# Retention's output blocks: group norm and gate product split over VectorE, ScalarE and GpSimd

## The reference, cut to what matters

```python
def head_groupnorm(y):
    mu = jnp.mean(y, axis=-1, keepdims=True)
    var = jnp.mean(jnp.square(y - mu), axis=-1, keepdims=True)
    return (y - mu) * lax.rsqrt(var + EPS)
...
    y, r_new = retention(q, k, vr, r0, chunk)
    y = head_groupnorm(y).reshape(B, T, R_V_WIDTH).astype(h.dtype)
    b = jax.nn.silu(gr) * y
```

## Time and profile before

| | |
|---|---|
| median of 3 runs | 1591.9 us (1589.27 to 1594.05) |
| the profiled execution's own time | 1587.36 us |
| its span | 1585.8 us |
| TensorE busy | 1550.2 us, 98% |
| VectorE busy | 882.9 us, 56% |
| ScalarE busy | 270.4 us, 17% |
| GpSimd busy | 62.9 us, 4% |
| output blocks, layer 0 | 357.4 to 414.6 us |
| output blocks, layer 1 | 1133.9 to 1191.1 us |

### The profile page before, as it was taken

The page is one execution under the profiler, slowest core; times in us unless marked ns, Lnnn a source line. Parts: engine busy times, 40 slices in busy tenths (PEclk is TensorE's granted clock), DMA queues, the critical chain, the costliest instruction groups (busy, mean ns, idle before and its releaser), DMA issues.

```text
span 1585.8 us, 24952 instructions
## 1 busy us (share of the span) xinstructions
PE 1550.2 (98%) x10010; PEld 1067.3 (67%) x10010; DVE 882.9 (56%) x1832; ACT 270.4 (17%) x556; POOL 62.9 (4%) x107
## 2 busy tenths in 40 slices
PE   6999999999999989999999999999999999999997
PEld 3999887775797544444449999886649965444443
DVE  2776864665752634344458768556485535434436
ACT  3110000112200421111131100011121033111111
POOL 0000000001001100000000000000010011000000
PEclk9999999999999999999999999999999999999999
DMA  9834665688843899999984437537886457999993
GB/s 396 334 111 160 261 271 226 268 342 329 334 160 113 317 366 422 420 421 421 422 352 153 161 142 286 193 127 307 335 342 249 160 224 275 416 419 421 422 420 138
DMA packets 49811, 461.43 MB, mean 291 GB/s; under 512 B 5968, under 2 KB 6224, under 8 KB 10144
## 3 DMA queue, kind: packets, MB, share of 16 engines
q1 hardware_dynamic: 44656, 414.38, 65.9%
q10 hardware_dynamic: 3456, 37.75, 5.7%
q0 software_dynamic: 1584, 7.69, 1.2%
HBM read 415.88 MB, written 43.91 MB: 290 GB/s over the span
## 4 chain that ended last, share of the span: by engine, by line
PE 86%; issue 8%; DMA 2%; DVE 1%; ACT 1%; POOL 1%; SPq 0%; POOLq 0%; DVEq 0%; ACTq 0%
PE ps L810 86%; DMA ring<-stream 1%; DMA ovd<-sorted_rows 1%; DMA sorted_rows<-work,packed_rows 1%; ACT work L1292 0%; POOL kzm L751 0%; POOL rstd L719 0%; POOL sorted_rows L771 0%; DVE rope L1611 0%; DVE hT L2187 0%; POOLq L718 0%; SPq L685 0%; DVEq L1555 0%; ACT hT L1292 0%; ACT modp L1292 0%
## 5 line engine op out<-in xcount | busy, mean ns | idle before, releaser
L810 PE MATMUL ps<-work,ring 128*128 128x144 f32 (+1 forms) x2624 | 358.2, 298 | 0.0
L810 PEld LDWEIGHTS ps<-work,ring 128*128 128x128 f32 x2624 | 341.0, 190 | 13.6 <-DVE ring L1653 0.2
L810 PE MATMUL ps<-ring,work 128*64 128x512 f32 x1472 | 323.9, 595 | 1.4 <-ACT work L1292 1.4
L810 PEld LDWEIGHTS ps<-ring,work 128*64 128x64 f32 x1472 | 106.6, 137 | 202.5 <-issue 202.4
L1292 ACT ACTIVATE work<-ps 128x256 f32<-128x256 f32 (+5 forms) x228 | 97.2, 433 | 720.9 <-PE ps L810 679.9
L810 PE MATMUL ps<-ring,hT 128*32 128x128 f32 (+2 forms) x1776 | 169.9, 312 | 3.0 <-ACT hT L1292 3.0
L810 PE MATMUL ps<-hT,ring 128*128 128x144 f32 (+1 forms) x1024 | 165.6, 317 | 0.0
L810 PEld LDWEIGHTS ps<-hT,ring 128*128 128x128 f32 x1024 | 145.8, 190 | 16.6 <-issue 3.6
L810 PE MATMUL ps<-work 128*128 128x288 f32 (+3 forms) x608 | 152.1, 393 | 3.4 <-DVE hT L2161 2.6
L810 PEld LDWEIGHTS ps<-ring,hT 128*32 128x32 f32 (+1 forms) x1776 | 126.1, 132 | 39.4 <-issue 26.5
L810 PEld LDWEIGHTS ps<-work 128*128 128x128 f32 (+1 forms) x608 | 100.6, 185 | 54.0 <-issue 26.9
(11 more groups left out here) (224 smaller groups left out, 1129.6 us busy)
## 6 DMA issues: line engine op xcount, KB each, us to landing
ring<-stream SPq DMA_DIRECT2D x194, 1024.0 KB, 10.4
ring<-stream SPq DMA_DIRECT2D x95, 2048.0 KB, 8.7
state_sample_out<-ring ACTq DMA_DIRECT2D x16, 2048.0 KB, 7.4
state_out<-prm ACTq DMA_DIRECT2D x8, 512.0 KB
work<-sorted_rows SPq DMA_DIRECT2D x6, 512.0 KB, 6.5
prm<-params SPq DMA_DIRECT2D x1, 2608.5 KB, 27.5
prm<-params POOLq DMA_DIRECT2D x1, 2608.5 KB, 16.7
cst<-consts SPq DMA_DIRECT2D x1, 1651.0 KB, 20.8
```

The source lines that it names most:

```text
L810: return nc.tensor.matmul(out, lhsT, rhs, start=start, stop=stop, **k)
```

## The change

VectorE keeps the statistics of all nine blocks and no longer multiplies out of PSUM. GpSimd's `inverse_root` also computes `centre` = -mean * rstd, with one more instruction ahead and one more, behind a second drain, at its end. ScalarE computes y * rstd + centre out of PSUM into `normal` (the buffer `modp`, two halves in turn) in `normalise`, and this is now what frees the block's bank. GpSimd multiplies the gate by that in `gate_rows` for n = 3 to 9; VectorE does it for the last two (n = 10 and 11), behind ysum's statistics. `inverse_root(n)` waits until block n-2 was normalised. `normalise(n)` waits until block n-2's gate product is done and, for n = 11, also block 10's.

```diff
--- before.py
+++ after.py
@@ -351,6 +351,7 @@
 VARS = 3 + 2 * HEADS + 1
 LN_DONE = 3
 B_DONE = 2 * HEADS + 1
+BY_VECTOR = LN_DONE + 2 * HEADS - 1
 NORMS = 2 * DEPTH
 SAMPLES = slice(SEQ, TOK)
 TTILES = ((0, P), (1, P), (2, NS))
@@ -383,6 +384,7 @@
         stats = sb("stats", [P, 2, 6])
         moments = sb("moments", [P, 4, 2])
         rstd = sb("rstd", [P, 2])
+        centre = sb("centre", [P, 2])
         kz = sb("kz", [P, 2, DK])
         scT = sb("scT", [P, 3, P])
         kzs = sb("kzs", [P, DK])
@@ -445,6 +447,16 @@
         sums_u = sums_of(work[:, QK_AT + 12 * RIDE:QK_AT + 12 * RIDE + KT * TOK], KT // 2, RIDE)
         sums_b = sums_of(work[:, SG_AT:SG_AT + 2 * KT * TOK], KT, RIDE)
         rope_flat = rope.rearrange("p a t -> p (a t)")
+        normal = modp
+
+        def normed_of(l, n):
+
+            head, c = (n - LN_DONE) // 2, (n - LN_DONE) % 2
+            return (l, "ysample") if head == HEADS else (l, ("y" if c else "r1", head), f"y{c}")
+
+        def gate_of(n):
+            head, c = (n - LN_DONE) // 2, (n - LN_DONE) % 2
+            return sgs if head == HEADS else sg[:, c, head * DV:head * DV + DV]
         kzm_flat = kzm.rearrange("p a d -> p (a d)")
 
         def partial(step):
@@ -712,11 +724,22 @@
             def inverse_root(l, n):
                 pool.wait_ge(var_ready, l * VARS + n + 1)
                 if n >= 5:
-                    pool.wait_ge(b_ready, l * B_DONE + n - 4)
+                    wait_reads(pool, [normed_of(l, n - 2)])
                 m = n % 2
+                pool.tensor_tensor(centre[:, m:m + 1], C("novr")[:, 0:1], moments[:, m, 0:1], ALU.subtract)
                 pool.tensor_tensor(rstd[:, m:m + 1], moments[:, m, 1:2], C("eps"), ALU.add)
                 pool.drain()
-                pool.tensor_tensor(rstd[:, m:m + 1], rstd[:, m:m + 1], C("half"), ALU.pow).then_inc(rstd_ready, 1)
+                pool.tensor_tensor(rstd[:, m:m + 1], rstd[:, m:m + 1], C("half"), ALU.pow)
+                pool.drain()
+                pool.tensor_tensor(centre[:, m:m + 1], centre[:, m:m + 1], rstd[:, m:m + 1], ALU.mult).then_inc(rstd_ready, 1)
+
+            def gate_rows(l, n):
+
+                if n == 3:
+                    pool.wait_ge(bent, BENT_AT[l, ("gr", 3)] + 1)
+                wait_reads(pool, [normed_of(l, n)])
+                rows = gate_of(n)
+                pool.tensor_tensor(rows, rows, normal[:, n % 2, :], ALU.mult).then_inc(b_ready, 1)
 
             for l in range(DEPTH):
                 if l > 0:
@@ -749,11 +772,10 @@
                             if b >= 2:
                                 wait_made(pool, (l, ("st", b - 2), f"1{HEADS - 1}"))
                             pool.tensor_tensor(kzm[:, b % 2, :], kzs[:, :], C("zetas")[:, b:b + 1].broadcast_to([P, DK]), ALU.mult).then_inc(kzm_ready, 1)
-                    elif kind == "r1":
+                    elif kind in ("r1", "y"):
                         inverse_root(l, n_var)
-                        n_var += 1
-                    elif kind == "y":
-                        inverse_root(l, n_var)
+                        if n_var < BY_VECTOR:
+                            gate_rows(l, n_var)
                         n_var += 1
                     elif kind == "ysum":
                         inverse_root(l, n_var)
@@ -1328,6 +1350,15 @@
                 wait_reads(act, [(l, step, "m4")])
                 apply(c21, c21, func).then_inc(bent, 1)
 
+            def normalise(l, n):
+
+                out = wait_made(act, normed_of(l, n))
+                if n >= LN_DONE + 2:
+                    act.wait_ge(b_ready, l * B_DONE + min(n - LN_DONE - 1, BY_VECTOR - LN_DONE) + (n > BY_VECTOR))
+                act.wait_ge(rstd_ready, l * VARS + n + 1)
+                m = n % 2
+                taken(apply(normal[:, m, :], out[:, :], ACT.Identity, scale=rstd[:, m:m + 1], bias=centre[:, m:m + 1]), normed_of(l, n))
+
             def load_sqrt():
 
                 apply(spare[:, :], C("eps"), ACT.Sqrt)
@@ -1434,11 +1465,7 @@
                         if kind == "r1":
                             if i >= 1 and i - 1 not in LATE_FINAL[l]:
                                 store_final(l, i - 1)
-                        c = 0 if kind == "r1" else 1
-                        wait_reads(act, [(l, step, f"y{c}")])
-                        act.wait_ge(rstd_ready, l * VARS + n_var + 1)
-                        rows = sg[:, c, i * DV:i * DV + DV]
-                        apply(rows, rows, ACT.Copy, scale=rstd[:, n_var % 2:n_var % 2 + 1]).then_inc(b_ready, 1)
+                        normalise(l, n_var)
                         n_var += 1
                     elif kind == "fout":
                         finals = [n for name, n in STEPS[l] if name == "fout"]
@@ -1454,9 +1481,7 @@
                     elif kind == "ysum":
                         if 3 not in LATE_FINAL[l]:
                             store_final(l, 3)
-                        wait_reads(act, [(l, "ysample")])
-                        act.wait_ge(rstd_ready, l * VARS + n_var + 1)
-                        apply(sgs, sgs, ACT.Copy, scale=rstd[:, n_var % 2:n_var % 2 + 1]).then_inc(b_ready, 1)
+                        normalise(l, n_var)
                         n_var += 1
                     elif kind == "bts":
                         out = wait_made(act, (l, step, "t"))
@@ -2056,12 +2081,6 @@
                         settle()
                         out = wait_made(dve, key)
                         moments_of([out[:, :]], n_var, l)
-                        settle()
-                        rows = sg[:, c, i * DV:i * DV + DV]
-                        if step == ("r1", 0):
-
-                            dve.wait_ge(bent, BENT_AT[l, ("gr", 3)] + 1)
-                        taken(dve.scalar_tensor_tensor(rows, out[:, :], moments[:, n_var % 2, 0:1], rows, ALU.subtract, ALU.mult), key)
                         n_var += 1
                     elif kind == "st":
                         state = cut(ring[LOAD_AT[l, step] % RING][:, :], HEADS, 2, DV)
@@ -2074,10 +2093,13 @@
                         settle()
                         out = wait_made(dve, (l, "ysample"))
                         moments_of([out[:, :]], n_var, l)
-                        settle()
+                        n_var += 1
+                        dve.wait_ge(bent, BENT_AT[l, ("gr", 3)] + 1)
                         wait_reads(dve, [(l, ("gr", n), "s") for n in range(4)])
-                        taken(dve.scalar_tensor_tensor(sgs, out[:, :], moments[:, n_var % 2, 0:1], sgs, ALU.subtract, ALU.mult), (l, "ysample"))
-                        n_var += 1
+                        for n in range(BY_VECTOR, n_var):
+                            wait_reads(dve, [normed_of(l, n)])
+                            rows = gate_of(n)
+                            dve.tensor_tensor(rows, rows, normal[:, n % 2, :], ALU.mult).then_inc(b_ready, 1)
                     elif kind == "bt" and i % 2 == 1:
                         out = wait_made(dve, (l, step, "t"))
                         tt, q = i // 4, i % 4
```

## The result

The changed kernel takes 1601.49 us (median of 4 runs, 1599.71 to 1601.85) beside 1590.86 us for the kernel before on the same chip: a ratio of 1.0063, 95% interval 1.0049 to 1.0077, so 7.8 to 12.2 us slower. A second set of runs gave 1.0063 again (1.0049 to 1.0076). The forecast was 1604.8 us, 12.9 us slower, with a range of 1598 to 1611. The profiled execution has a span of 1598.1 us, 12.3 us over that of before.

The account below looks back on a forecast made before the run. The bound was taken as a round trip from TensorE's outer(1) through VectorE, GpSimd and ScalarE back to TensorE. 2.26 + 2.24 + 1.94 = 6.44 us a layer, 12.9 in all, on 1591.9 gave 1604.8 us, range 1598 to 1611.

Parts of the forecast that it names:

- Read the stalls, not the busy shares: Rival at outer(1) of st(6), st(7): VectorE's relief decides, returning at most 2 x 1.58 = 3.2 us; chance 0.05.
- the stretches: Output-block spans, one a layer, from st(5)'s outer(0) to the first transpose; each forecast 6.4 us longer, the rest unchanged.
- Step 1: r1(1)'s longer root and ScalarE's normalisation free bank 5 later; outer(0) of st(6) starts 0.93 us late.
- Step 2: y(1)'s root waits behind r1's gate product on GpSimd, delaying normalisation and key copies; outer(1) of st(6) 2.26 us later.
- Steps 3 and 4: Second head: the same trip through r1(2) and y(2) makes outer(1) of st(7) 4.50 us late, another 2.24.
- Step 5: After st(7): the chain through r1(3), y(3) and ysum starts the transposes 1.94 us late; sum 6.44 us a layer.
- the rule that speaks for more: VectorE with two SBUF inputs and GpSimd reading SBUF lock each other out; at VectorE's last two products, some 0.2 us a layer.
- The prices: Instruction times assumed: GpSimd's 128x512 gate product 1.26 us, ScalarE's normalisation with scale and bias 0.78 us.
- the 0.80 us that the prediction sets beside it: The Trainium skill's formula price for ScalarE's normalisation; with it the sum would be 0.3 us higher.
- The delay is not taken up behind: Against the rival that a later stage, paced by transfers, absorbs TensorE's lateness: 1592 to 1596 us, chance 0.08.
- The sum against the median: Whole kernel: 12.9 us added to 1591.9 us on the scale of the runs' median gives 1604.8 us.
- the branch that was given 0.75: The main forecast of delay through both layers' output blocks: 5.2 to 8.4 us a layer, 1602 to 1609 us.

Follow-up runs that it names:

- experiment 6: Kernel before without VectorE's nine products out of PSUM a layer, banks released by the statistics, output blocks left out: 1587.99 us, ratio 0.9981.
- experiment 7: Changed kernel with y's root ahead of r1's product and kt(2), kt(3) moved ahead of r1(1), r1(2) in the steps: 1589.58 us, ratio 0.9993.
- experiment 1: Changed kernel with GpSimd making y's root ahead of r1's gate product: 1593.55 us, ratio 1.0015 to the kernel before.
- experiments 2 and 3: Changed kernel with GpSimd's gate products cut to one column: 1595.5 us, ratio 1.0024; with each made twice: 1609.68 us, ratio 1.0123.
- experiment 5: Kernel before with only GpSimd's longer inverse root added, its centre result unused: 1592.63 us, ratio 1.0012.
- experiment 8: Kernel before with only kt(2) and kt(3) moved ahead of r1(1) and r1(2) in the list of steps: 1591.09 us, ratio 1.0004.
- experiments 4 and 5: The former: changed kernel with ScalarE copying kt(2), kt(3) ahead of normalising y(1), y(2), 1598.32 us, ratio 1.0044; the latter: see experiment 5.
- experiment 9: Kernel of experiment 7 with VectorE also taking block n = 9's product, with its own semaphore: 1587.87 us, ratio 0.9980 to the kernel before.

## Why the prediction was right

- *Read the stalls, not the busy shares.* Right. The relief of VectorE is capped at the stalls, 3.2 us forecast; measured were 3.0 by the whole time and 2.5 by the stretches (experiment 6).
- *Step 1, r1's bank 0.93 us late.* Right to 0.01 us in the profile, and shown by experiment 7, where another bank in its place removes it.
- *Step 2, y's root behind r1's product.* This carries the loss. outer(1) came 2.13 us later than before (11.68 to 13.81 us after st(5)'s outer(0)); forecast 2.26. Experiment 1 removes it with the order alone, experiments 2 and 3 scale it. The root took 1.35 to 1.36 us (394.23 to 395.58) and not 1.42: two neighbouring GpSimd instructions overlap by 0.05 (390.68 + 0.19, and the next begins at 390.82). Like the whole sum, this step errs a little on the high side.
- *Steps 3 and 4.* Right: 4.26 us for 4.50 at outer(1) of st(7).
- *Step 5, the end.* Right: 6.29 and 6.15 us a layer for 6.44. The transposes came 2.03 and 1.87 us behind TensorE's own pace, for 1.94. The clash of the rule that speaks for more was there, and ysum's root took 0.46 us longer by it; but its normalisation also had to wait for VectorE's product, which ended 0.05 us before, so it cost next to nothing.
- *The prices.* Right: 1.266 us for the product (1.26) and 0.777 for the normalisation (0.78); the 0.80 us that the prediction sets beside it is 0.02 too long here.
- *The delay is not taken up behind.* Right by the profiles: the span grew by what the two stretches grew.
- *The sum against the median.* 12.9 us were forecast and the ratio says 7.8 to 12.2, where the profiled executions differ by 12.3. So 1601.49 us is inside the stated range of 1598 to 1611, but 0.5 us below 1602 to 1609, the inner range of the branch that was given 0.75. Of the 3.3 us between 1604.8 and 1601.49, 1.0 is the base (1591.9 was taken, 1590.86 is the median beside it) and 0.5 the sum. The last 1.7 come from the profiled executions: that of before lies 3.5 us under the median beside it (1587.36 and 1590.86), that of the changed kernel only 1.8 under its own. The mean granted clock of each execution points the same way. It is 0.999 in the profiled execution of before and 0.992 to 0.998 in the others for which the record has it; it is 0.997 in the profiled one of the changed kernel and 0.993 to 0.996 in its others. Some profiles show where: 0.83 in 20 to 30 us in experiment 5 and 0.66 in 570 to 580 us in experiment 1, where both profiles of before and after have 1.00. How much of the last 2 us this makes is not shown, and they stay open.

Not foreseen was TensorE's clock; the last section has it.

## What to carry to other kernels

When work moves from a loaded engine to an idle one, ask what stands behind it in the idle engine's program and who waits for that: here a product of 1.26 us, of no hurry itself, stood between two roots on which PSUM banks hung, and its place alone cost 7.6 us of 10.0 (9.3 of 12.4 in the stretches). Relief of an engine gives back at most the stalls that it causes on the bound engine, so measure those before paying for it. And where a ring of banks holds the bound engine, look at which tile the first-needed bank belonged to: moving a tile whose reader is quick into that place cost nothing here, gave 3.5 us where the bank was late (experiment 7) and nothing that whole times show where it was not (experiment 8).

## What the runs showed of the hardware

**TensorE's clock fell behind the long waits.** In the changed kernel, layer 0, the weight loads had been idle for 2.97 us before outer(1) for the second time, and the products for 2.09; then (columns as in the windows above)

```profile
408.00:410.00 2.00, 1.28 (x9) 0.35 (x9) 0.11 (x1) 0.62 (x2) 1.24 (x1) 0.88 1.01 434
410.00:413.00 3.00, 3.00 (x7) 1.45 (x5) 2.83 (x5) 0.00 (x0) 0.00 (x0) 0.51 0.68 289
```

the granted clock is 0.51, the 1.2 GHz level, from 410 to 413 us. The weight loads of r1(3) and y(3) stand 0.86 us apart in it, and 0.43 behind it, up to the first of the next step:

```profile
411.01 0.34 PEld L832 LDWEIGHTS ps<-work,scT 128*128 128x128 f32 x1 [0.52 <-issue]
411.87 0.34 PEld L832 LDWEIGHTS ps<-work,scT 128*128 128x128 f32 x1 [0.52 <-issue]
...
413.27 0.19 PEld L832 LDWEIGHTS ps<-work,scT 128*128 128x128 f32 x1 [0.24 <-issue]
413.70 0.19 PEld L832 LDWEIGHTS ps<-hT,ring 128*128 128x128 f32 x1 [0.24 <-issue]
```

In layer 1 the same happened a head earlier (0.66 from 1180 to 1185 us), and the repeat of the changed kernel shows both. With the product made twice, whose weight loads were idle for up to 4.21 us, it came once in layer 0 and twice in layer 1. In the kernel before, whose idle times there are 1.81 us at most, and in experiments 4 and 5 with 2.28 us at most, the clock stays at 1.00 in the stretches. That the waits are the cause is not shown: the clock also fell elsewhere, in some profiles and not in others (0.66 from 570 to 580 us in experiment 1, 1.00 there before and after).

It cost little here. In layer 0 outer(1)'s own products took 1.34 us instead of 1.14, VectorE's updates began 1.32 us after outer(1) instead of 1.16, and the transposes came 13.33 us after it, where it is 13.17 in layer 1. In layer 1 the next outer(0) came 1.12 us later than in layer 0, but outer(1) had to wait anyway and came as in layer 0 (25.24 and 25.23 us after st(5)'s outer(0)).

**A GpSimd instruction waited out a VectorE one.** The root's last product, one column, takes 0.19 us. Beside VectorE's product with both operands in SBUF:

```profile
419.61 0.69 DVE L2102 TENSOR_TENSOR work<-work,modp 128x512 f32<-128x512 f32 x1 [2.86 <-ACT modp L1314]
419.70 0.65 POOL L734 TENSOR_TENSOR centre<-centre,rstd 128x1 f32<-128x1 f32 x1
420.46 0.78 ACT L1314 ACTIVATE modp<-ps,centre,rstd 128x512 f32<-128x512 f32 x1 [0.99 <-POOL centre L734]
```

it took 0.65 us (419.70 to 420.35) and ended 0.05 us after VectorE's (419.61 to 420.30). In layer 1 it took 0.65 again. In experiment 9 the same thing on the chain:

```profile
413.14 0.69 DVE L2108 TENSOR_TENSOR work<-work,modp 128x512 f32<-128x512 f32 x1
413.16 0.72 POOL L736 TENSOR_TENSOR centre<-centre,rstd 128x1 f32<-128x1 f32 x1
...
414.00 0.78 ACT L1318 ACTIVATE modp<-ps,centre,rstd 128x512 f32<-128x512 f32 x1 [1.22 <-POOL centre L736]
```

0.72 us instead of 0.19, which moved y(3)'s normalisation by 0.5 us. In layer 1 of that kernel the root's product began 0.05 us ahead of VectorE's (1189.64, 1189.69) and kept its 0.19 us, and GpSimd's next one took 0.66. Beside the state updates, which read one operand in PSUM, GpSimd's products kept their length: the two of experiment 1 took 2.51 us from 393.26 on while VectorE ran its updates from 393.82 on. The Trainium skill ("SBUF — State Buffer", SBUF: two separate sides) states that a VectorE instruction with two SBUF inputs and a GpSimd one that reads SBUF exclude each other: the one that starts first keeps the shared ports for its whole length. This trace agrees, with these numbers.
